# A two-block transformer kernel: the second block's Q, K and V projected in one stage, with Q's norm moved into the softmax's scale

## What is computed

```python
def rmsnorm_2(x, g):
    y = x32 * lax.rsqrt(jnp.mean(x32 * x32, axis=-1, keepdims=True) + NORM_EPS)
    return y * g

# layer 0, differential attention: 16 half heads of 64, for all 768 tokens
q, k, v = split(t @ w_in, 3)
q = rmsnorm_2(q.reshape(..., 16, 64), q_norm)
k = rmsnorm_2(k.reshape(..., 16, 64), k_norm)
q, k = apply_axial_rope(q, cos, sin), apply_axial_rope(k, cos, sin)   # 512 tokens only
p = softmax(q @ k.T * 64 ** -0.5)
o = (p[:, :, 0] - lam * p[:, :, 1]) @ v
y = (rmsnorm_2(o, subln) * (1 - lambda_init)) @ w_out
# layer 1, grouped attention: 8 query heads of 128, 2 key heads; queries for 512 tokens only
```

## Time and profile before

| what | value |
|---|---|
| median of 3 runs | 4993.71 us (4993.27 to 4996.43) |
| the profiled execution's own time | 4992.37 us |
| its span | 4990.9 us |
| TensorE, matmuls | 4485.6 us busy, 90% of the span |
| VectorE, ScalarE, GpSimd | 40%, 30%, 11% |
| mean granted TensorE clock | 0.929 of full speed |
| second block's layer 0, from the norm's start to attention's start | 2955.4 to 3318.9 us |
| second block's layer 1, the same | 4215.0 to 4413.4 us |

### The profile page before, as it was taken

How to read it: one execution, slowest core, us unless ns; L and a number is a source line. 1 busy time by engine, 2 the same in 40 slices (tenths; PEclk the granted TensorE clock), 3 DMA queues, 4 the chain that set the end, 5 groups by cost and what they waited for, 6 DMA issues and landing times. The chain is left out here.

```text
span 4990.9 us, 76816 instructions
## 1 busy us (share of the span) xinstructions
PE 4485.6 (90%) x33574; PEld 3470.8 (70%) x33574; DVE 1996.0 (40%) x2982; ACT 1511.2 (30%) x2667; POOL 556.8 (11%) x401
## 2 busy tenths in 40 slices
PE   6799999799968898999799869888889998888999
PEld 5676896577756766987577647465678886466877
DVE  4536334455334436344455242337331132234232
ACT  2533233322233432332323232136221122233221
POOL 1215100011001115000010000102000000032000
PEclk9899999899978998999899979799899998889999
DMA  3022002144322122012244211010011111101222
GB/s 136 30 102 68 29 5 97 64 169 169 114 67 83 47 95 75 4 41 97 85 169 158 91 47 47 21 34 1 30 47 63 64 60 51 47 9 39 93 89 85
DMA packets 97534, 351.87 MB, mean 71 GB/s; under 512 B 9904, under 2 KB 13488, under 8 KB 95792
## 3 DMA queue, kind: packets, MB, share of 16 engines
q1 hardware_dynamic: 86432, 313.01, 18.3%
q10 hardware_dynamic: 10768, 33.95, 1.8%
...
## 5 line engine op out<-in xcount | busy, mean ns | idle before, releaser
L290 DVE TENSOR_TENSOR wlo<-ring,whi 128x1024 fp32r<-128x1024 f32 x494 | 626.3, 1268 | 2060.7 <-ACT whi L280 2060.6
L280 ACT CAST whi<-ring 128x1024 fp32r<-128x1024 f32 x494 | 517.7, 1048 | 2512.0 <-PE ps L332 2108.1
L329 PE MATMUL ps<-h_hi,whi 128*128 128x512 f32 x1552 | 648.7, 418 | 48.2 <-DVEq L228 27.4
L332 PE MATMUL ps<-h_hi,wlo 128*128 128x512 f32 x1552 | 623.4, 402 | 0.0
L330 PE MATMUL ps<-h_lo,whi 128*128 128x512 f32 x1552 | 622.4, 401 | 0.0
L329 PE MATMUL ps<-hm_hi,whi 128*128 128x512 f32 (+1 forms) x1408 | 508.8, 361 | 50.3 <-POOL spread L1947 40.7
L330 PE MATMUL ps<-hm_lo,whi 128*128 128x512 f32 (+1 forms) x1408 | 483.2, 358 | 0.0
L329 PEld LDWEIGHTS ps<-h_hi,whi 128*128 128x128 f32 x1552 | 297.8, 192 | 198.6 <-issue 68.5
L332 PE MATMUL ps<-hm_hi,wlo 128*128 128x512 f32 (+1 forms) x1408 | 423.4, 358 | 0.0
L329 PEld LDWEIGHTS ps<-hm_hi,whi 128*128 128x128 f32 x1408 | 268.2, 190 | 134.2 <-POOL spread L1947 41.1
L329 PE MATMUL ps<-ac_hi,whi 128*128 128x512 f32 x880 | 332.3, 378 | 23.9 <-DVE ac_lo L484 23.1
...
## 6 DMA issues: line engine op xcount, KB each, us to landing
...
ma<-m_spill ACTq DMA_DIRECT2D x2, 2048.0 KB, 10.2
...
```

What stands on the lines that cost most here:

```text
L280: self.A.copy(self.hi[k % 2][:], raw).then_inc(self.s_cut_hi.h, 1)
L290: self.V.tensor_tensor(self.lo[k % 2][:], raw, self.hi[k % 2][:].bitcast(F32), ALU.subtract).then_inc(self.s_cut_lo.h, 1)
L329: T.matmul(ps[:, b, 0:cw], hi, xh(q, c0, cw), start=q == 0, stop=False, skip_group_check=True)
L332: m = T.matmul(ps[:, b, 0:cw], lo, xh(q, c0, cw), start=False, stop=q == kt - 1, skip_group_check=True)
```

## The change

`project_heads` and `values_token_major` become one function, `project`, without a fence between them.

- Q is copied from PSUM times its gain and is turned without being normed. The reciprocal roots of its variances are kept on 96 partitions (three groups of 256 tokens; 64 partitions in layer 1), transposed once by TensorE, multiplied by the attention's constant scale and put into `self.rq`, one column of 128 tokens per token tile and head. The attention's exp and the negated maximum take their scale from there instead of from a constant.
- K is copied times its gain and turned in the same way; its norm is applied to the turned tile between V's steps.
- `head_sum` sums by groups of 256 tokens, each into its own 32 rows of PSUM; `spread` is made from columns of the identity, so GpSimd's selector goes. `norm_outputs` is changed in the same way.
- V's bank copies are shared out between ScalarE and VectorE, three each; the next row waits bank by bank.
- Lambda's chain is put into the ticks of columns 0, 2, 3 and 5.
- The tables are loaded a stage ahead: the first ones in the first block's last layer, the second ones at the start of layer 0's attention.

```diff
-               ("band", 256), ("invf", 1), ("sel", 30), ("sel_all", 30), ("rows8", 8), ("eps", 1)):
+               ("band", 256), ("invf", 1), ("sel", 46), ("sel_all", 46), ("rows8", 8), ("eps", 1)):
...
+        if layer == L - 1:
+            self.load_tables("tab64")
...
+        self.rq = self.sml[:, 0:96]
...
-    def values_token_major(self, width, n_rows):
...
-    def make_spread2(self):
...
-    def project_heads(self, q_segs, n_k, gains, rot, sel, width, ready):
...
-        scale = DIFF_HD ** -0.5
+        scale = lambda s, q: self.rq_of(steps[s][1], 2 * steps[s][0] + q)
...
-            A.activation(e(s, q), scores_of(s, q), ACT.Exp, bias=st[:, 1:2], scale=scale,
+            A.activation(e(s, q), scores_of(s, q), ACT.Exp, bias=st[:, 1:2], scale=scale(s, q),
...
-            V.tensor_scalar(st[:, 1:2], st[:, 0:1], -scale, None, ALU.mult).then_inc(self.s_anm.h, 1)
+            V.tensor_scalar(st[:, 1:2], st[:, 0:1], scale(s, q), -1.0, ALU.mult, ALU.mult).then_inc(self.s_anm.h, 1)
...
-        e = self.s_load.take(16) + 16
-        self.V.wait_ge(self.s_load.h, e)
-        self.G.wait_ge(self.s_load.h, e)
+        self.s_load.take(16)
+    def wait_tables(self):
+        self.V.wait_ge(self.s_load.h, self.s_load.n)
...
+    def project(self, q_segs, n_k, gains, rot, sel, width, ready, scale, v_width, v_rows, first, lam=False):
...
+        groups = (wd(0) // 256, 3)
+        rows = [self.view(f"hrows{x}", TB2 + 2 * T2 + x * 256, 256)[0:32 * groups[x], :] for x in range(2)]
...
+        place = [0, 1, 5, 4, 2, 3]
...
+        def head_sum(n):
+            at = CONST[sel] + 14 - 2 * local(n)
+            x = n >= n_q
+            T.wait_ge(self.s_hsq.h, b_sq + n + 1)
+            if lam and n == n_q:
+                T.wait_ge(self.s_lam2.h, self.s_lam2.n)
+            for g in range(groups[x]):
+                m = T.matmul(ps[32 * g:32 * g + 32, 6 + x, 0:256], con[:, at:at + 32],
+                             sq[n % 2][:, 256 * g:256 * g + 256], start=local(n) == 0, stop=local(n) == size(n) - 1,
+                             skip_group_check=True)
+            m.then_inc(self.s_hsum.h, 1)
...
+        def turn(n):
+            T.wait_ge(self.s_pcopy.h, b_pc + n + 1)
+            if n >= 2:
+                T.wait_ge(self.s_hsin.h, b_sin + n - 1)
+            if n == N - 1:
+                T.wait_ge(self.s_rq.h, b_rq + 1)
+            T.matmul(ps[:, rot_bank(n), :], rot, tile(n)[:, 0:S], start=True, stop=True,
+                     skip_group_check=True).then_inc(self.s_hrot.h, 1)
+        def rows_turned():
+            T.wait_ge(self.s_hrows.h, b_rows + 1)
+            n = 32 * groups[0]
+            for b in range(2):
+                m = T.transpose(ps[:, 6, 256 + b * P:256 + b * P + n], rows[0][:, b * P:(b + 1) * P],
+                                self.c("ident")[0:n, 0:n])
+            m.then_inc(self.s_rqt.h, 1)
...
+        def spread(k):
+            if k == 0:
+                T.wait_ge(self.s_hrows.h, b_rows + 2)
+                T.wait_ge(self.s_hsin.h, b_sin + N)
+            else:
+                T.wait_ge(self.s_scaled.h, b_scl + k)
+            for g in range(3):
+                for half in range(2):
+                    one = CONST["ident"] + 32 * g + 2 * k + half
+                    pick = con[0:96, one:one + 1].to_broadcast([96, 64])
+                    m = T.matmul(ps[64 * half:64 * half + 64, 6 + g // 2, 256 * (g % 2):256 * (g % 2) + 256], pick,
+                                 rows[1], start=True, stop=True, skip_group_check=True)
+            m.then_inc(self.s_hspr.h, 1)
...
+        def pe_tick(n):
+            if n > 0:
+                head_sum(n - 1)
+                turn(n - 1)
+            if n == n_q + 1:
+                rows_turned()
...
+        def act_tick(n, value):
+            A.wait_ge(self.s_mm.h, value)
+            for (c0, cw), b in zip(segs(n), banks_of(n)):
+                i = A.activation(tile(n)[:, c0:c0 + cw], ps[:, b, 0:cw], ACT.Identity, scale=gain(n))
+            i.then_inc(self.s_pcopy.h, 1)
+            if n >= 2:
+                A.wait_ge(self.s_hsum.h, b_sum + n - 1)
+            for (c0, cw), b in zip(segs(n), banks_of(n)):
+                i = A.activation(sq[n % 2][:, c0:c0 + cw], ps[:, b, 0:cw], ACT.Square)
+            i.then_inc(self.s_hsq.h, 1)
...
+        def query_scales():
+            V.wait_ge(self.s_rqt.h, b_rqt + 1)
+            n = groups[0]
+            src = ps[:, 6, 256:512].rearrange("p (b x) -> p b x", b=2)[:, :, 0:32 * n]
+            dst = self.rq[:, 0:32 * n].rearrange("p (g b k) -> p b g k", b=2, k=16)
+            V.tensor_scalar(dst, src.rearrange("p b (g k) -> p b g k", k=32)[:, :, :, 0:16], scale, None,
+                            ALU.mult).then_inc(self.s_rq.h, 1)
...
+        def pe():
+            for n, col in enumerate(cols):
+                free(n)
+                self.column(col, self.h2h, self.h2l, segs(n), banks_of(n), ready if n == 0 else None)
+                pe_tick(n)
+            for s, st in enumerate(steps):
+                r, q = divmod(s, DT)
+                hi, lo = self.halves_of(st)
+                for k, tt in enumerate(place):
+                    if s == 0 and k == 0:
+                        evicted(N - 2)
+                    if s == 0 and k == 2:
+                        T.wait_ge(self.s_hsin.h, b_sin + N - 1)
+                    if s == 0 and k == 4:
+                        evicted(N - 1)
+                    if q == 0 and r > 0:
+                        T.wait_ge(*((self.s_v2d.h, b_vd + 3 * (r - 1) + k // 2 + 1) if k % 2 else
+                                    (self.s_v2.h, b_v + 3 * (r - 1) + k // 2 + 1)))
+                    toks, o = slice(tt * P, (tt + 1) * P), ps[:, tt, 0:v_width * P]
+                    T.matmul(o, self.h2_hi[:, q, toks], hi, start=q == 0, stop=False, skip_group_check=True)
+                    T.matmul(o, self.h2_hi[:, q, toks], lo, start=False, stop=False, skip_group_check=True)
+                    m = T.matmul(o, self.h2_lo[:, q, toks], hi, start=False, stop=q == DT - 1, skip_group_check=True)
+                m.then_inc(self.s_mm.h, 1)
+                if s == 0:
+                    head_sum(N - 1)
+                    turn(N - 1)
+                if first <= s < first + n_k:
+                    spread(s - first)
...
+        def act_v():
+            for s, st in enumerate(steps):
+                r, q = divmod(s, DT)
+                if q == DT - 1:
+                    A.wait_ge(self.s_mm.h, st.value)
+                    for k in range(0, 6, 2):
+                        out(A.copy, k, r).then_inc(self.s_v2.h, 1)
+                if st.at + st.n == PIECE:
+                    self.act_cuts(self.ahead(st.cut))
+                if s == 0:
+                    root(1)
...
+        def dve_v():
+            for s, st in enumerate(steps):
+                r, q = divmod(s, DT)
+                if q == DT - 1:
+                    V.wait_ge(self.s_mm.h, st.value)
+                    for k in range(1, 6, 2):
+                        out(V.tensor_copy, k, r).then_inc(self.s_v2d.h, 1)
+                if st.at + st.n == PIECE:
+                    self.dve_cuts(self.ahead(st.cut))
+                if s == 0:
+                    var(1)
+                    rope(N - 1)
+                    inverse(1)
+                if first <= s < first + n_k:
+                    k = s - first
+                    V.wait_ge(self.s_hspr.h, b_spr + k + 1)
+                    V.wait_ge(self.s_hrope.h, b_rope + n_q + k + 1)
+                    V.tensor_tensor(tile(n_q + k)[:, 0:S], tile(n_q + k)[:, 0:S], ps[:, 6, :], ALU.mult)
+                    V.tensor_tensor(tile(n_q + k)[:, S:T2], tile(n_q + k)[:, S:T2], ps[:, 7, 0:CTX],
+                                    ALU.mult).then_inc(self.s_scaled.h, 1)
...
-        self.load_tables("tab64")
...
+        self.wait_tables()
+        self.project(SEG2, DT, (self.p2("dq"), self.p2("dk")), self.c("rot_ax64"), "sel", 64,
+                     lambda q: T.wait_ge(self.s_nlo.h, b_lo + q + 1), DIFF_HD ** -0.5, 4, 2, 2, lam=True)
+        self.load_tables("tab128")
...
-        e_spr = self.make_spread2()
-        rows = self.view("hrows0", TB2 + 2 * T2, T2)[0:2 * DT, :]
+        rows = self.view("hrows0", TB2 + 2 * T2, 256)[0:96, :]
...
+                for g in range(3):
+                    m = T.matmul(ps[32 * g:32 * g + 32, 6, 0:256], con[:, at:at + 32],
+                                 sq[h % 2][:, 256 * g:256 * g + 256], start=h == 0, stop=h == DT - 1,
+                                 skip_group_check=True)
...
+                for g in range(3):
+                    one = CONST["ident"] + 32 * g + 2 * h
+                    m = T.matmul(ps[:, 2 * (h % 3) + g // 2, 256 * (g % 2):256 * (g % 2) + 256],
+                                 con[0:96, one:one + 1].to_broadcast([96, P]), rows, start=True, stop=True,
+                                 skip_group_check=True)
...
-        self.A.wait_ge(self.s_nhi.h, self.s_nhi.n)
```

(9 more changed lines are left out.)

329 lines of the change are left out of this document (112 added, 217 removed).

## The result

| | before | after |
|---|---|---|
| median | 4993.49 us (4 runs, 4990.98 to 4996.43) | 4828.64 us (4 runs, 4823.99 to 4834.49) |
| ratio | | 0.967 (95% interval 0.9654 to 0.9687) |
| profiled execution's own time | 4992.37 us | 4826.08 us |
| its span | 4990.9 us | 4824.6 us |
| mean granted TensorE clock | 0.929 | 0.944 |

The forecast was 4836 (4818 to 4862); the change makes the kernel 165 us faster. The page's busy times, against the earlier trace rows: TensorE does 88.5 us less, its share of the span hardly moves.

A forecast was written before the change was run, and what follows sets the result against it. The prediction took TensorE's column work plus serial chains as the bound. Gains of 12.3, 76.2, 8.5, 56.4 and 8.8 less 5.5 made 156.7 us off 4992.4, giving 4835.7 and a forecast of 4836 us, range 4818 to 4862.

The forecast's parts named there:

- its own case: Whole kernel: the forecast's mechanisms hold and the time falls between 4825 and 4845 us; chance 0.68.
- Entry: First column behind each second-block layer's norm: no selector or table wait, gaining 12.3 us in layer 0, 8.5 in layer 1.
- the 1.5 us that I took off: Layer 1's first column: deducted from a 10 us gain because the low clock may last into the next column.
- Layer 0 to attention: Layer 0, end of column 0 to attention: TensorE's list sums to 240.8 us against 317.0, gaining 76.2.
- The 1.28 us for exp's table load: Layer 0, last matmul to first scores: exp's table load was expected to come behind the first maximum.
- Layer 1 to attention: Layer 1, end of column 0 to attention: 97.9 us against 154.3, gaining 56.4.
- norm_outputs: norm_outputs: sums, reciprocal, variance and root get shorter, spreads keep the same columns; gain 8.8 us.
- The third rival: Exp's pointer hides and norm_outputs' spreads run at full clock: 5.5 and 8 us more, 4822; chance 0.08.
- Attention: Attention in both layers: exp reads its scale through a second pointer, costing 0 to 13 us, taken as 5.5.
- serial spreads: K's spreads between V steps: halves run one after the other, 2.9 us instead of 1.6, 4849 us; chance 0.12.
- the entry that gains nothing: Layer entries: TensorE still starts late, losing 20.8 us, 4857; or ScalarE holds a column, 4842; chance 0.09.
- the clock rival: K's and V's stretches: small fp32 matmuls lower TensorE's clock, 5175 us at the worst; chance 0.02.

The follow-up runs named there:

- after_tables_at_entry: The changed kernel with the tables' loads put back behind each layer's norm, instead of a stage ahead; 4832.01 us.
- after_old_layout: The changed kernel with constants as long as before and those the first block reads at their old places; 4818.98 us.

## Why the prediction was right, and where only the sum was

4836 was forecast and 4828.6 came, in the range and inside its own case (4825 to 4845), whose mechanisms held:

- **Entry.** 12.2 and 9.6 us against 12.3 and 8.5. The low clock took little from the next column of layer 1 (5.80 us there, 5.61 in after_tables_at_entry), so most of the 1.5 us that I took off should have stayed in.
- **Layer 0 to attention.** 80.3 against 76.2. Columns took 10.00 us, not 10.20: 3.0 us over 15 of them. Spreads came at 1.51 (1.63 with what is around them) for the 1.6 taken; made to share partitions they took 2.80. The Trainium skill (TensorEngine Tiling, Key Properties) has tiles of one mode run in parallel, and the trace agrees. Whatever its drain at a change of mode costs here lies inside the 1.63 us, and no run shows it apart. The handover, 3.85 forecast, was 3.90 of TensorE idleness. The 1.28 us for exp's table load was wrong: the load runs beside the first scores.
- **Layer 1 to attention.** 57.0 against 56.4; Q columns of 7.22 us for 7.38 in the sum. There the table load is on the path.
- **norm_outputs.** This is the term of the sum that was mis-sized: 8.8 forecast, 17.8 measured. The sums gave 5.2 us (4.6 forecast), the gap with variance, root and reciprocal 4.1 (4.2 forecast), the spreads 8.5 (nothing forecast). The sentence that failed is "Spreads have the same columns" with half clock taken for them. The third rival ("more than I count") held this case at 8 us; of its two halves this one came, the hidden pointer did not. Behind it the projection's first columns started at full clock too, which gave 2.4 of the 3.8 us in the next line of the table (88.7 to 86.3 us up to swiglu's norm). Neither is safe: in after_old_layout norm_outputs takes 27.2 us instead of 25.5 and the projection's first matmuls are at half clock.
- **Attention.** -5.5 forecast; -4.0 in layer 0, and 2.5 in layer 1 by the run with the constant scale. That run puts the whole at 5.7 us between profiled second blocks (1844.0 against 4821.8 - 2983.5 = 1838.3). I took 73 ns for a pointer, from a square, and put VectorE's pointer in the negated maximum at nothing; it costs 60 ns on the same loop. The two exps show 996 - 906 = 90 ns. By the Trainium skill (ScalarE: Activation LUTs, What ACT_TABLE_LOAD costs) each pointer operand adds about 93 ns, and here the trace agrees with it better than with my row.
- **First block.** No term; it cost 9.6 us in the profile, and two kernels with nothing but longer constants put the price of those at 6.2 and 6.4 us of the whole. I read the wider selection tables in the diff and gave them no price.

Between the profiled executions the forecast was 9.4 us too small, 166.1 against 156.7: +9 (norm_outputs), +4 (columns), +4 (projection and swiglu), +2 (layer 1 and attention) and -10 (first block) partly cancel. Between the medians 7.4 are left, because the changed kernel's median lies 2.6 us above its profiled execution and not 1.3, and because the prediction wrote 4836 where its own sum, 4835.7 and 1.3, is 4837.0. That the number came so near is in part luck: with the constants as long as before the same change measured 4818.98, at the low edge of the range. The rivals: serial spreads were excluded by a run that made them serial; the entry that gains nothing and the clock rival find no row for them, as the entries gained 12.2 and 9.6 us and both projections run at clock 1.00 behind column 0.
